# u and v rows of a mixture of experts side by side: one 8 KB gather per choice for three of four token tiles

## The chip, the cores and the metric

One core of a Trainium2 chip. The time is device microseconds of one execution, median over runs: 4290.01 us (4275.37, 4290.01, 4290.02).

## The reference

Two transformer blocks on 512 tokens of width 1024; the second ends with a layer of single experts (PEER), which is all that the change touches. For a tile of 128 tokens:

```
q = t @ wq                          # per head, two halves of 128
v1,i1 = top_k(q1 @ k1.T, 16); v2,i2 = top_k(q2 @ k2.T, 16)
score, ci = top_k(v1[:,None]+v2[None,:], 16)       # of 256 sums
expert = i1[ci // 16] * 128 + i2[ci % 16]          # one of 16384
w = softmax(score) * gelu(u_tab[expert] . t)       # u_tab: 16384 x 1024
y = sum over 8 heads x 16 choices of w * v_tab[expert]
```

So each token has 128 choices, and each choice reads one row of 1024 f32 (4 KB) of u and one of v. After it come a scaled residual and a layer norm.

## The kernel before

It is one program per engine, with the order written out by hand and semaphores between engines. Each stage names its steps (`pe.V.at("dot", n)` is "VectorE has finished step dot n of stage peer"). The 512 tokens are four tiles; tile 0 is prepared (attention output, merge, norm, query product, selection) while the last attention runs, tiles 1 to 3 together behind it.

`FETCH` (L2502) is the order of all 1024 row gathers, and also the order of work: `("pu", i, j)` is u row of choice j of tile i, `("pv", i, j)` its v row. Tile 0's first 64 u rows go alone, then one v row comes per four u rows, and from u row 128 on five v rows per four u rows, until the v rows have caught up. So tile 1's u rows run beside tile 0's v rows, and v rows trail u rows by up to 112.

A gather (L2752, on POOL's queue) brings one row per partition, 128 rows of 4 KB, 512 KB, into one of `PLACES`: 7 places for the first 144 gathers, then 19 (12 more in the panels of the weight w_pq+, free once the query product of tiles 1 to 3 is done). It waits until the last row of that place is used: a u row by its dot, a v row by its matmuls.

`in_order` (L2670) is run by every engine with its own parts: at each row r it first issues the gathers whose places come free by r (on POOL), waiting with `advance` while the selection of their head isn't `ready`, then does the row's own work, then `advance(r)`: 2 steps of the selection for r < 128, later 2 and 1 in turn, and from r >= 30 on every third turn one step of the rest of the tail for tiles 1 to 3 (`others`).

- VectorE, u row (L2782): one multiply and sum of the row with the token tile (the dot). After 16 of them five small instructions make the gelu's polynomial, and ScalarE's sigmoid stands between them (L2715, L2792).
- ScalarE, v row (L2721): a diagonal 128x128 of the weights w, in one of 4 buffers.
- TensorE, v row (L2705): diagonal times row, two halves of 512 columns, summed in PSUM; the profile shows four matmuls of 128x512 f32 per v row.
- Selection on VectorE (L2609 to L2664): some 27.5 steps per head, among them L2611 (needs ScalarE's copy of the scores, L2586) and the softmax (needs L2592). The query product of tiles 1 to 3 is L258, 16 groups of 16 matmuls.
- At each tile's last v row (L2802) VectorE makes the residual and the norm.

Of the kernel before, what the change touches and what calls it, by code (L numbers as in the profile page):

```python
# [8 lines left out]
U32 = mybir.dt.uint32  # L9
# [90 lines left out]
def build(nc, d, out):  # L100
    ctx = ExitStack()
    with ctx:
# [2398 lines left out]
        BL = 16  # L2501
        FETCH = []  # L2502
        done_v = 0
        for n_ in range(1, 513):
            FETCH.append(("pu", (n_ - 1) // 128, (n_ - 1) % 128))
            goal = 0 if n_ < 64 else (n_ - 64) // 4 if n_ < 128 else 16 + (n_ - 128) * 5 // 4 if n_ < 512 else 512
            while done_v < goal:
                FETCH.append(("pv", done_v // 128, done_v % 128))
                done_v += 1
        ROWS = len(FETCH)  # L2510
        PLACES = [piece(o_cs + 1024), piece(o_ka + 1024), piece(o_ka + 2048), piece(o_cs), MIXf[:, 0:1024], piece(o_ht + 1024), piece(o_ka)]
        FEW = len(PLACES)
        PLACES += [panel("w_pq+", c)[:, 1024 * j:1024 * j + 1024] for c in (1, 2, 3) for j in range(4)]
        MANY = len(PLACES)
        FROM = 144
        SPOT = [n % FEW if n < FROM else (n - FROM) % MANY for n in range(ROWS)]
        NTH, PREV, uses, user_row = [], [], [0] * MANY, [-1] * MANY
        for n_ in range(ROWS):
            uses[SPOT[n_]] += 1
            NTH.append(uses[SPOT[n_]])  # L2520
            PREV.append(user_row[SPOT[n_]])
            user_row[SPOT[n_]] = n_
        NUMBER = {f: n for n, f in enumerate(FETCH)}
        s_row_in = [sem(f"s_in{j}") for j in range(MANY)]

        def fetched(f):
            return s_row_in[SPOT[NUMBER[f]]], 16 * NTH[NUMBER[f]]

        def row(f):
            return PLACES[SPOT[NUMBER[f]]]  # L2530

# [6 lines left out]
        EXU = [piece(o_end + 128 * j, 128).bitcast(U32) for j in range(4)]  # L2538
        DOT = [piece(o_end + 512 + 128 * j, 128) for j in range(2)]
# [69 lines left out]
        def select_vector(v, asked, ready):  # L2609
# [12 lines left out]
            for i in range(4):  # L2622
                for h in range(8):
# [11 lines left out]
                    pe.V.own(v).tensor_copy(I1F, I1).then_inc(*pe.V.step())  # L2635
# [4 lines left out]
                    for half in (0, 1):  # L2640
# [3 lines left out]
                        else:  # L2644
# [10 lines left out]
                                                     op1=ALU.add).then_inc(*pe.V.step("sel", i, h))  # L2655
                    yield
# [13 lines left out]
        def in_order(e, part, select, gather=lambda n: None):  # L2670
# [12 lines left out]
            for r in range(ROWS):  # L2683
                while n < ROWS and PREV[n] < r:
                    tab, i, j = FETCH[n]
                    while tab == "pu" and (i, j // 16) not in ready:
                        advance(r)
                    gather(n)
                    n += 1
                yield FETCH[r]  # L2690
                advance(r)
# [35 lines left out]
        YY, XHR = MIXf[:, 1024:2048], MIXf[:, 2048:3072]  # L2727
        s_late, s_xhr = sem("s_late"), sem("s_xhr")

        def rows_gpsimd(g):  # L2730
            def gather(n):
                tab, i, j = FETCH[n]
                if PREV[n] >= 0:
                    tab0, i0, j0 = FETCH[PREV[n]]
# [4 lines left out]
                elif SPOT[n] in (1, 2):  # L2739
                    g.wait_ge(*tl.V.at("rows"))  # L2740
                elif SPOT[n] == 3:
                    g.wait_ge(*tl.V.at("bias"))
                elif SPOT[n] == 4:
                    g.wait_ge(*tl.P.at("mx", 0, 1))
                elif SPOT[n] == 5:
                    g.wait_ge(*tl.P.at("o", 0, 1, 0))
                elif SPOT[n] == 6:
                    g.wait_ge(s_xh[0], 16)
                elif SPOT[n] >= FEW:
                    g.wait_ge(*tl.P.at("q", 1, 4 * (1 + (SPOT[n] - FEW) // 4) + 3))  # L2750
                g.wait_ge(*pe.V.at("sel", i, j // 16))
                g.indirect_dma_start(PLACES[SPOT[n]], None, d[tab], bass.IndirectOffsetOnAxis(ap=EXU[i][:, j:j + 1], axis=0)  # L2752
                                     ).then_inc(s_row_in[SPOT[n]], 16)
# [3 lines left out]
            for f in in_order(g, tail_gpsimd, select, gather):  # L2757
                if f == ("pv", 0, 24):
# [320 lines left out]
```

## Time and profile before

| | |
|---|---|
| median of 3 runs | 4290.01 us |
| profiled execution: span from first to last instruction | 4287.8 us |
| TensorE busy | 3534.2 us (82%) |
| VectorE busy | 2141.1 us (50%) |
| POOL busy | 1437.5 us (34%) |
| gathers: 512 u rows, 512 v rows | mean 1070 and 1100 ns on POOL |
| dots (L2782) | 512, mean 1221 ns |
| matmuls of v rows (L2705) | 2048, 1029.6 us |

The page gives no other time for the profiled execution than its span. Shares are means over stages with different limits; the slices and the tables by stage show which engine is full where.

### The profile page before, as it was taken

How to read it: one execution, taken by the hardware profiler on the slowest of the kernel's cores; microseconds unless marked ns; L12 is line 12 of the kernel's file. 1: busy time of each engine (PE TensorE's matmuls, PEld its weight loads, DVE VectorE, ACT ScalarE, POOL GpSimd, SP SyncE). 2: the span in 40 equal slices, each digit the busy share in tenths (PEclk: the TensorE clock that was granted, in tenths of full speed). 3: DMA queues.
4: the chain of work that ended last, by engine and by line, in shares of the span. 5: the costliest groups of instructions: out<-in, count | busy, mean ns of one | idle time of the engine just before them, and what ended most of it. 6: DMA issues, size and time to landing. Idle time of an engine off the chain costs nothing.

```text
span 4287.8 us, 33127 instructions
## 1 busy us (share of the span) xinstructions
PE 3534.2 (82%) x10814; PEld 1820.1 (42%) x10814; DVE 2141.1 (50%) x4648; ACT 910.5 (21%) x1890; POOL 1437.5 (34%) x1337
## 2 busy tenths in 40 slices
PE   8377999999997999979999875678777777777776
PEld 4244544444453564456544563234333333333232
DVE  0557234421013567746344458764678776334432
ACT  1234411000032225622110322111122212111111
POOL 0214400000000006400000023354777776777774
PEclk9668999999999989979899987889898898988998
DMA  3010111333211113201212456675998999999996
GB/s 153 8 50 1 57 62 69 157 149 129 95 59 54 59 54 106 81 35 62 101 39 98 154 188 224 236 281 200 375 350 324 353 369 334 366 371 363 369 360 244
DMA packets 171912, 765.15 MB, mean 178 GB/s; under 512 B 19256, under 2 KB 19256, under 8 KB 160224
## 3 DMA queue, kind: packets, MB, share of 16 engines
q0 software_dynamic: 157904, 580.06, 36.8%
q1 hardware_dynamic: 13824, 182.97, 11.4%
q8 instruction: 88, 1.44, 0.1%
q14 instruction: 80, 0.66, 0.0%
q10 hardware_dynamic: 16, 0.02, 0.0%
HBM read 744.08 MB, written 18.89 MB: 178 GB/s over the span
## 4 chain that ended last, share of the span: by engine, by line
PE 50%; DVE 18%; issue 10%; POOL 5%; DMA 3%; ACT 3%; another core or an unknown queue 2%; POOLq 0%; DVEq 0%; ACTq 0%
PE ps L252 14%; PE ps L258 11%; DVE arena L2782 7%; PE ps L1416 6%; PE ps L1346 5%; POOL arena L2752 4%; PE ps L2705 4%; PE ps L1722 2%; PE ps L220 2%; DMA arena<-in_pu,arena 1%; DMA arena<-in_pv,arena 1%; PE ps L1709 1%; DVE arena L2613 1%; DVE arena L2619 1%
## 5 line engine op out<-in xcount | busy, mean ns | idle before, releaser
L2705 PE MATMUL ps<-arena 128*128 128x512 f32 x2048 | 1029.6, 658 | 395.5 <-issue 195.0
L2705 PEld LDWEIGHTS ps<-arena 128*128 128x128 f32 x2048 | 411.3, 208 | 991.1 <-issue 881.0
L2782 DVE CUSTOM_DVE_ANT_0 arena<-arena 128x1024 f32<-128x1024 f32 x512 | 622.6, 1221 | 367.3 <-DMA arena<-in_pu,arena 337.6
L252 PE MATMUL ps<-arena 128*128 128x512 f32 (+1 forms) x1768 | 755.9, 588 | 32.0 <-ACT arena L2271 24.4
L2752 POOL DMA_INDIRECT arena<-in_pu,arena x512 | 547.7, 1070 | 422.7 <-issue 98.1
L2752 POOL DMA_INDIRECT arena<-in_pv,arena x512 | 563.1, 1100 | 204.3 <-issue 127.1
L258 PE MATMUL ps<-arena 128*128 128x512 f32 (+2 forms) x1408 | 529.5, 537 | 3.1 <-DVE arena L1263 0.9
L252 PEld LDWEIGHTS ps<-arena 128*128 128x128 f32 x1768 | 337.9, 192 | 435.7 <-issue 430.6
L258 PEld LDWEIGHTS ps<-arena 128*128 128x128 f32 x1408 | 267.6, 191 | 262.0 <-issue 216.8
L220 PE MATMUL ps<-arena 128*128 128x128 f32 x1046 | 194.5, 321 | 206.0 <-ACT arena L812 49.8
L2721 ACT ACTIVATE arena<-arena 128x128 f32<-128x128 f32 x512 | 192.8, 397 | 751.1 <-PE ps L2705 360.6
L1416 PE MATMUL ps<-arena 128*128 128x512 f32 x640 | 293.6, 606 | 20.1 <-ACT arena L1802 12.8
L263 POOL TENSOR_TENSOR arena<-arena 128x1 f32<-128x1 f32 (+7 forms) x38 | 61.3, 1615 | 722.7 <-DVE arena L630 311.0
L220 PEld LDWEIGHTS ps<-arena 128*128 128x128 f32 x1046 | 141.1, 163 | 288.8 <-issue 146.7
L1440 POOL DMA_DIRECT2D aside<-arena x20 | 10.7, 534 | 661.5 <-ACT arena L1430 661.5
L1346 PE MATMUL ps<-arena 128*128 128x512 f32 x512 | 221.5, 593 | 1.4 <-DVE arena L1380 1.4
L1416 PEld LDWEIGHTS ps<-arena 128*128 128x128 f32 x640 | 118.6, 194 | 147.7 <-issue 129.4
L1072 POOL TENSOR_SCALAR arena<-arena 128x128 f32<-128x128 f32 (+3 forms) x96 | 111.3, 1170 | 157.6 <-DVE arena L1103 89.0
L1246 POOL DMA_DIRECT2D x_spill<-arena x1 | 0.6, 573 | 463.8 <-DVE arena L1377 463.8
L1346 PEld LDWEIGHTS ps<-arena 128*128 128x128 f32 x512 | 96.7, 190 | 125.7 <-issue 123.4
L1722 PEld LDWEIGHTS ps<-arena 128*128 128x128 f32 x896 | 119.0, 209 | 30.6 <-issue 17.2
L1722 PE MATMUL ps<-arena 128*128 128x64 f32 x896 | 118.1, 289 | 5.9 <-DVE arena L1918 5.8
(342 smaller groups left out, 3399.5 us busy)
## 6 DMA issues: line engine op xcount, KB each, us to landing
arena<-in_w_in SPq DMA_DIRECT2D x27, 2048.0 KB, 8.9
arena<-in_w_ada SPq DMA_DIRECT2D x12, 2048.0 KB, 8.0
arena<-in_w_ff_in SPq DMA_DIRECT2D x8, 2048.0 KB, 12.5
arena<-in_w_ff_out SPq DMA_DIRECT2D x8, 2048.0 KB, 12.5
arena<-in_w_pq SPq DMA_DIRECT2D x8, 2048.0 KB, 8.5
aside<-arena POOLq DMA_DIRECT2D x20, 512.0 KB, 4.5
arena<-in_w_at SPq DMA_DIRECT2D x4, 2048.0 KB, 8.9
arena<-in_w_o SPq DMA_DIRECT2D x4, 2048.0 KB, 8.7
```

The costliest lines, as they stand in the source:

```text
L220: return t.transpose(ps, src, ID[0:src.shape[0], 0:src.shape[0]])
L252: x = t.matmul(PS[:, b, 0:n], hT[:, k, i * 128:(i + 1) * 128], w[:, k, :], start=k == 0, stop=k == nk - 1)
L258: x = t.matmul(PS[:, b, 0:n], w[:, k, f * 128:(f + 1) * 128], hT[:, k, 0:n], start=k == 0, stop=k == nk - 1)
L263: return g.tensor_tensor(o, o, MH[0:o.shape[0], 0:o.shape[-1]], ALU.pow)
L1072: g.tensor_scalar(probs(i, h), probs(i, h), r[:, 6 + h:7 + h], None, ALU.mult).then_inc(*at1.G.step("scaled", i, h))
L1346: x = t.matmul(PS[:, 4 * c + i, :], AT[:, 8 * kk + k, 128 * i:128 * i + 128], w[:, k, :], start=kk == 0 and k == 0, stop=kk == 3 and k == 7)
L1416: x = t.matmul(PS[:, b, :], l, r, start=k == 0, stop=k == 7)
L1722: x = t.matmul(PS[:, b, 64 * c:64 * c + 64].rearrange("p (n t) -> p n t", t=w), WL[lv % 4][:, o:o + 128], sides(WL[lv % 4][:, o:o + 128], ...
L2705: x = t.matmul(PS[:, b + c, :], DG[n % 4], row(f)[:, 512 * c:512 * c + 512], start=j == 0, stop=j == 127)
L2721: a.activation(DG[n % 4], ID, ACT.Copy, scale=GS[i][:, j:j + 1]).then_inc(*pe.A.step("dg", n))
L2752: g.indirect_dma_start(PLACES[SPOT[n]], None, d[tab], bass.IndirectOffsetOnAxis(ap=EXU[i][:, j:j + 1], axis=0)).then_inc(s_row_in[SPOT[n]] ...
L2782: v.tensor_tensor_reduce(row(f), row(f), TT[i], 1.0, 0.0, ALU.mult, ALU.add, DOT[i % 2][:, j:j + 1]).then_inc(*pe.V.step("dot", 128 * i + j))
```

## The change

- The tables are laid side by side (`uv`, 16384 rows of 2048 f32). For tiles 1 to 3 one gather per choice brings the 8 KB row into one of 14 places of 8 KB (`PAIRS`): u in the first half, v in the second. For tile 0 the same table is seen as 32768 rows of 4 KB (`HALVES`), u at index 2e, v at 2e + 1 (`EXV`), in 7 places (`CELLS`).
- The order is now a list of work (`WORK`), apart from the list of gathers: tile 0's u rows with v rows as before up to u row 127, then its remaining 112 v rows alone, then for tiles 1 to 3 u row n and v row n - 10 (`LAG`) in turn. There are 256 + 384 = 640 gathers. A place of 8 KB is freed by the v row's matmuls. Eight of the 14 places lie on regions that tile 0's places or other buffers use, with waits for their last users.
- The gelu blocks are 8 choices for tiles 1 to 3 (16 for tile 0), with one small instruction fewer.
- Some waits and loads beside it move to other rows (late rows at v row 80 and 112 of tile 0, residual at 116 instead of 100), and two buffers move.

```diff
-        BL = 16
-        FETCH = []
...
-            goal = 0 if n_ < 64 else (n_ - 64) // 4 if n_ < 128 else 16 + (n_ - 128) * 5 // 4 if n_ < 512 else 512
...
-        FROM = 144
-        SPOT = [n % FEW if n < FROM else (n - FROM) % MANY for n in range(ROWS)]
...
+        BLOCK = (16, 8, 8, 8)
+        LAG = 10
+        UV = d["uv"]
+        HALVES = UV.rearrange("e (s n) -> (e s) n", s=2)
+        WORK = []
+        done_v = 0
+        for n_ in range(1, 129):
+            WORK.append(("pu", 0, n_ - 1))
+            while done_v < (n_ - 64) // 4:
+                WORK.append(("pv", 0, done_v))
+                done_v += 1
+        WORK += [("pv", 0, j_) for j_ in range(done_v, 128)]
+        for n_ in range(384 + LAG):
+            if n_ < 384:
+                WORK.append(("pu", 1 + n_ // 128, n_ % 128))
+            if n_ >= LAG:
+                WORK.append(("pv", 1 + (n_ - LAG) // 128, (n_ - LAG) % 128))
...
+        PAIRS = [panel("w_pq+", c)[:, 2048 * j:2048 * j + 2048] for c in (1, 2, 3) for j in range(2)]
+        PAIRS += [piece(o, 2048) for o in (o_va + 1024, o_ka + 2048, o_qa + 2048, o_ka, o_cs, W0, o_t + 2048, o_ht)]
+        MANY = len(PAIRS)
+        SHARED = {7: (2,), 9: (6, 1), 10: (3, 0), 11: (4,), 13: (5,)}
+        FETCH = [f for f in WORK if f[1] == 0]
+        SPOT = [n % FEW for n in range(256)]
+        FETCH += [("uv",) + f[1:] for f in WORK if f[1] and f[0] == "pu"]
+        SPOT += [FEW + n % MANY for n in range(384)]
...
@@ selection, vector @@
+                    if i == 0:
+                        pe.V.own(v).tensor_scalar(EXV[:, hs], EXU[0][:, hs], 1, None, ALU.add).then_inc(*pe.V.step("selv", h))
@@ in_order @@
-                while n < ROWS and PREV[n] < r:
+                while n < FETCHES and FREED[n] < r:
...
-                    while tab == "pu" and (i, j // 16) not in ready:
+                    while tab != "pv" and (i, j // 16) not in ready:
@@ gather @@
+                if i == 0:
+                    g.wait_ge(*(pe.V.at("sel", 0, j // 16) if tab == "pu" else pe.V.at("selv", j // 16)))
+                    x = (EXU[0] if tab == "pu" else EXV)[:, j:j + 1]
+                    g.indirect_dma_start(CELLS[k], None, HALVES, bass.IndirectOffsetOnAxis(ap=x, axis=0)).then_inc(s_row_in[k], 16)
+                else:
+                    g.wait_ge(*pe.V.at("sel", i, j // 16))
+                    g.indirect_dma_start(PAIRS[k - FEW], None, UV, bass.IndirectOffsetOnAxis(ap=EXU[i][:, j:j + 1], axis=0)
+                                         ).then_inc(s_row_in[k], 16)
@@ rows_vector @@
+                        pe.V.own(v).scalar_tensor_tensor(out=y, in0=x, scalar=0.044715, in1=x, op0=ALU.mult, op1=ALU.mult
+                                                         ).then_inc(*pe.V.step())
+                        pe.V.own(v).scalar_tensor_tensor(out=y, in0=y, scalar=1.0, in1=x, op0=ALU.add, op1=ALU.mult
+                                                         ).then_inc(*pe.V.step("poly", i, j // bl))
@@ layout @@
-    a["pu"] = i["peer_u_2"][0]
-    a["pv"] = i["peer_v_2"][0]
+    a["uv"] = np.concatenate([i["peer_u_2"][0], i["peer_v_2"][0]], 1)
```

## Rows read from the trace of the kernel before

**Rows 1.** The page: DMA's busy tenths in 40 slices of 107.2 us.

```profile
DMA  3010111333211113201212456675998999999996
```

**Rows 2.** Window, us, busy us (x) of PE PEld DVE ACT POOL, clock, DMA share, GB/s.

```profile
2519.00:2891.00 372.00, 231.06 (x744) 129.22 (x745) 287.67 (x709) 65.29 (x133) 164.21 (x155) 0.81 0.72 244
2891.00:2964.00 73.00, 67.24 (x194) 36.01 (x193) 22.53 (x66) 12.19 (x27) 16.66 (x17) 1.00 0.32 108
...
3300.00:3600.00 300.00, 230.54 (x507) 99.16 (x506) 226.08 (x651) 61.29 (x157) 226.07 (x203) 0.89 0.95 353
3600.00:3900.00 300.00, 229.78 (x464) 92.24 (x462) 126.30 (x220) 47.50 (x126) 221.23 (x208) 0.88 0.97 363
3900.00:4245.00 345.00, 254.80 (x517) 100.87 (x516) 137.50 (x245) 51.16 (x137) 252.27 (x241) 0.91 0.97 364
```

**Rows 3.** The same windows for the gathers alone (L2752): POOL busy (count).

```profile
2519.00:2891.00 372.00, 157.55 (x144) 0.81 0.72 244
...
3600.00:3900.00 300.00, 220.04 (x206) 0.88 0.97 363
3900.00:4245.00 345.00, 251.10 (x239) 0.91 0.97 364
```

**Rows 4.** Timeline of POOL, unheld: start us, us, what [idle before <-releaser].

```profile
3532.43 0.94 POOL L2752 DMA_INDIRECT arena<-in_pu,arena  x1 [0.30 <-issue]
```

**Rows 5.** As rows 2: 16 KB rows (5:25), then 4 KB rows; the weight loads.

```profile
5.00:25.00 20.00, 10.44 (x44) 7.63 (x45) 5.92 (x9) 6.73 (x12) 1.02 (x1) 1.00 1.02 428
3000.00:3050.00 50.00, 34.81 (x69) 14.75 (x70) 29.24 (x84) 7.26 (x18) 35.07 (x34) 0.80 1.01 394
4100.00:4200.00 100.00, 71.82 (x148) 27.16 (x146) 41.31 (x75) 12.88 (x36) 73.96 (x72) 0.94 1.00 380
...
arena<-in_w_in SPq DMA_DIRECT2D x27, 2048.0 KB, 8.9
```

**Rows 6.** Timelines of POOL and of PE around the 144th gather.

```profile
2891.61 0.95 POOL L2752 DMA_INDIRECT arena<-in_pu,arena  x1 [7.96 <-DVE arena L2658]
...
2962.55 0.95 POOL L2752 DMA_INDIRECT arena<-in_pu,arena  x1 [25.94 <-PE ps L258]
...
2890.64 26.03 PE L258 MATMUL ps<-arena 128*128 128x384 f32 x80
```

**Rows 7.** DVE by line, 3300 to 3600 us; first and last of six dots.

```profile
L2782 DVE CUSTOM_DVE_ANT_0 arena<-arena 128x1024 f32<-128x1024 f32 x94 | 114.1, 1216 | 3.2 <-DMA arena<-in_pu,arena 2.3 <-issue 0.9
L2611 DVE MAX8 arena<-arena 128x8 f32<-128x128 f32 (+1 forms) x32 | 11.0, 342 | 44.0 <-ACT arena L2586 25.8 <-issue 14.6 <-remote 1.9
...
3427.97 1.21 DVE L2782 CUSTOM_DVE_ANT_0 arena<-arena 128x1024 f32<-128x1024 f32 x1
...
3440.99 1.22 DVE L2782 CUSTOM_DVE_ANT_0 arena<-arena 128x1024 f32<-128x1024 f32 x1
```

**Rows 8.** v rows on PE: L2705's matmuls to 2880 us; timelines at 2889, 3780.

```profile
2519.00:2880.00 361.00, 42.06 (x56) 13.50 (x56) 0.81 0.73 246
...
2888.85 1.95 PE L2705 MATMUL ps<-arena 128*128 128x512 f32 x4 [0.96 <-ACT arena L2721]
...
3779.95 3.75 PE L2705 MATMUL ps<-arena 128*128 128x512 f32 x4 [6.10 <-issue]
3784.21 25.04 PE L2705 MATMUL ps<-arena 128*128 128x512 f32 x56 [0.51 <-issue]
```

**Rows 9.** Timeline of the end: last gather, v rows, last DVE step.

```profile
4244.17 0.95 POOL L2752 DMA_INDIRECT arena<-in_pv,arena  x1 [0.30 <-issue]
...
4248.70 25.98 PE L2705 MATMUL ps<-arena 128*128 128x512 f32 x56 [1.98 <-ACT arena L2721]
...
4282.90 1.23 DVE L2815 TENSOR_TENSOR arena<-arena 128x1024 f32<-128x1024 f32 x1
```

**Rows 10.** A wait, 3300 to 3600 us (total, times, longest); the queues' instruction packets.

```profile
ACT arena L2586 <- remote: 37.2, 3, 21.1
...
q8 instruction: 88, 1.44, 0.1%
```

More of the change, by code:

```diff
@@ new lines, in build, with number, emptied @@
+        for n_ in range(FETCHES):
+            k_ = SPOT[n_]
+            PREV.append([held_by[k_]] if uses[k_] else [held_by[c] for c in SHARED.get(k_ - FEW, ())])
+            uses[k_] += 1
+            NTH.append(uses[k_])
+            held_by[k_] = FETCH[n_]
+        NUMBER = {f: n for n, f in enumerate(FETCH)}
+        s_row_in = [sem(f"s_in{j}") for j in range(FEW + MANY)]
+        def number(f):
+            return NUMBER[f if f[1] == 0 else ("uv",) + f[1:]]
+        def emptied(f):
+            return ("pu" if f[0] == "pu" else "pv",) + f[1:]
@@ L2526, in fetched @@
+        FREED = [max((WHEN[emptied(f)] for f in before), default=-1) for before in PREV]
         def fetched(f):
-            return s_row_in[SPOT[NUMBER[f]]], 16 * NTH[NUMBER[f]]
+            return s_row_in[SPOT[number(f)]], 16 * NTH[number(f)]
         def row(f):
-            return PLACES[SPOT[NUMBER[f]]]
+            n = number(f)
+            if f[1] == 0:
+                return CELLS[SPOT[n]]
+            o = 1024 * (f[0] == "pv")
+            return PAIRS[SPOT[n] - FEW][:, o:o + 1024]
@@ L2634, in select_vector @@
                     pe.V.named["used", i, h] = pe.V.n
-                    pe.V.own(v).tensor_copy(I1F, I1).then_inc(*pe.V.step())
+                    if i:
+                        pe.V.own(v).tensor_copy(I1F, I1).then_inc(*pe.V.step())
+                    else:
+                        pe.V.own(v).tensor_scalar(I1F, I1, 2.0, None, ALU.mult).then_inc(*pe.V.step())
                     v.tensor_tensor(CD.rearrange("p (a b) -> p a b", a=16), bc(V1[:, 0, :], 16), rep(V1[:, 1, :], 16), ALU.add
@@ L2732, in gather @@
                 tab, i, j = FETCH[n]
-                if PREV[n] >= 0:
-                    tab0, i0, j0 = FETCH[PREV[n]]
+                k = SPOT[n]
+                for tab0, i0, j0 in PREV[n]:
                     if tab0 == "pu":
@@ L2738, in gather @@
                         g.wait_ge(*pe.P.at("add", 128 * i0 + j0))
[L2739 to L2750, printed above, removed]
@@ L2751, in gather @@
-                g.wait_ge(*pe.V.at("sel", i, j // 16))
-                g.indirect_dma_start(PLACES[SPOT[n]], None, d[tab], bass.IndirectOffsetOnAxis(ap=EXU[i][:, j:j + 1], axis=0)
-                                     ).then_inc(s_row_in[SPOT[n]], 16)
+                if NTH[n] == 1:
+                    if k in (1, 2):
+                        g.wait_ge(*tl.V.at("rows"))
+                    elif k == 3:
+                        g.wait_ge(*tl.V.at("bias"))
+                    elif k == 4:
+                        g.wait_ge(*tl.P.at("mx", 0, 1))
+                    elif k == 5:
+                        g.wait_ge(*tl.P.at("o", 0, 1, 0))
+                    elif k == 6:
+                        g.wait_ge(s_xh[0], 16)
+                    elif k >= FEW:
+                        g.wait_ge(*tl.P.at("q", 1, (7, 7, 11, 11)[k - FEW] if k < FEW + 4 else 15))
+                    if k == FEW + 8:
+                        g.wait_ge(s_xh[1], 16)
+                        g.wait_ge(s_xh[2], 32)
+                    elif k == FEW + 12:
+                        g.wait_ge(*tl.V.at("tt", 3))
+                        g.wait_ge(*pe.V.at("dot", 127))
+                    elif k == FEW + 13:
+                        g.wait_ge(*pe.P.at("sc", 0, 3))
@@ L2797, in rows_vector @@
                     v.tensor_scalar(LATE[3], LATE[3], ALPHA, None, ALU.mult).then_inc(*pe.V.step())
-                if f and tab == "pv" and j == 100:
+                if f and tab == "pv" and j == 116:
                     v.wait_ge(s_xhr, 16 * (i + 1))
```

56 lines of the change are left out of this document (24 added, 32 removed).

## The prediction

> **What bounds the kernel now.** I read the page's slices first [rows 1]: DMA's tenths go from 5 to 7 up to 9 for the last 12 slices, from about 3000 us. So the last 1.3 ms are bound near DMA, and only the gathers that fill them are touched by the change. The table by stage [rows 2] gives the four stages: to 2891 us tile 0's u rows (DMA share 0.72); 2891 to 2964 with DMA at 0.32; then both tiles' rows with the selection beside them, DMA 0.95 and the vector engine (DVE) 0.75 busy; from 3600 DMA 0.97 and DVE only 0.40 to 0.42. The gathers by stage [rows 3]: 144 before 2891 us, then 880 until the last at 4244 us [rows 9], 1.54 us each with the hole at the start, and 1.45 us each after 3600 (445 in 645 us), that is 2.90 us for the two rows of a choice.
>
> Why not faster? Two things are close together. POOL needs 1.25 us per gather (0.94 and 0.30 between) when nothing holds it [rows 4], and 512 KB at the highest rate that gathers reach over 50 us (394 GB/s, a few plain loads among them) is 1.33 us [rows 5]. A POOL that is held for a few us can therefore never catch up. The hole at 2891: the gather after the 144th wants tile 1's first choices, which the order puts before tile 0's remaining v rows, and POOL waits for the selection (7.96 us) and for TensorE's query product (25.94 us) [rows 6]. In the third stage DVE, which works through choices in a fixed order, is the pace: 94 dots in 300 us, 3.19 us each, with almost no wait for DMA (3.2 us) but 44.0 us at L2611 for the score copy [rows 7].
>
> **The change part by part.** Up to the 144th gather nothing moves except 8 small DVE instructions (the v indices) and one fewer per block, about 0.2 us each: 2891 us stays.
>
> *A, tile 0's v rows by themselves.* 112 v rows now stand in a row with no dot beside them, and TensorE is what is busy. Before 2890.6 us it had done 15 v rows (56 matmuls up to 2880, 4 more at 2889, four a row) [rows 8]; to v row 120, whose place lets the first 8 KB gather start, 106 remain. A row costs 1.78 us back to back (56 matmuls in 25.04), 1.96 alone [rows 8]: 106 x 1.78 = 189. The query product of tiles 1 to 3 still has 10 groups of 16 matmuls (five take 26.03, 5.2 each) [rows 6], 52 us, a gap of 1 us at each (0.96 in [rows 8]), and I allow 4 us for score matmuls: 255 us, so v row 120 is done at 3146. DMA (106 x 1.33 = 141 us) and POOL hide beneath. The hole at 2891 goes, since no choice of tile 1 is asked for in this stretch; by the turn counts, 1.5 selection steps a row make 6 of tile 1's 8 heads ready by then. With 1.95 a row it is 3164, the upper end; the lower is 3141.
>
> *B, choices while DVE still selects.* DVE must first finish tile 0's end (12 us of v rows left, then its chain, 4274.7 to 4284.1 in the last tile [rows 9]): 3168. The selection of tiles 1 to 3 has 24 heads x 27.5 = 660 steps. Tile 1's first query product is asked for about row 135, and 1.5 steps in each of the 120 rows from there do 180. The other 480 come at 1.5 a turn: one turn in each of the first 10 choices, two in the others, so 155 more choices carry three steps each. In the packed stretch six dots start 2.60 us apart, with 3.4 steps each [rows 7]: the dot with its read-out 1.26, so a step 0.40. A choice is then 1.26 + 3 x 0.40 = 2.46, and a block of 8 adds 4 small instructions and the wait for the sigmoid, 1.7 us, 0.21 a choice: 2.67. Ten light choices at 1.9 and 155 at 2.67 end at 3168 + 19 + 414 = 3601. This is above DMA's pace (below), so DVE is the bound there. Lower end 2.5 (no waits); upper 3.19, as now, if the waits at L2611 stay.
>
> *C, the rest.* Fourteen places less the ten choices between a dot and its v row leave three or four 1 MB transfers in flight. DMA is then about 2 choices ahead of DVE: 217 remain. No row shows an indirect row of 8 KB. From one side: TensorE's weights come in rows of 16 KB (2048 KB over 128 partitions) at 428 GB/s [rows 5], 2.45 us for 1 MB. From the other: the rate of 4 KB rows with the chip's queues full, 394 and 380 GB/s [rows 5], 2.66 and 2.76; the average now is 2.90 [rows 3]. A price per row and one per byte fitted to 394 and 428 (256 rows a MB in 2.66 us, 64 in 2.45, so 128 in 2.52) say 2.52; I take 2.55. POOL has 1.25 us of work in that time and stops being a partner in the bound. Places: after block b's last dot its v rows start some 4 us later and take 8 x 1.98 us (229.78 us for 464 matmuls, four a row [rows 2]); the gather for the first freed place must be out within 6 x 2.55 = 15 us and is out after 8 or 9, the last within 33 and out after 22. So depth is enough at this clock. 217 x 2.55 = 553: last row lands at 4154; the tiles' residual loads, output stores and two tile ends add 8 (six transfers of 512 KB at 1.3 us): 4162.
>
> *The end.* Now the last gather goes out at 4244.2, but TensorE is 15 v rows behind and ends at 4274.7 [rows 9], and 13.1 us follow. Then: dot 1.3, small work 2, 8 v rows (first at half clock, 3.75, the rest 1.78) 16.2, and 13.1: 33 us. 4162 + 33 = 4195.
>
> *Waits for nothing in the program.* ACT stood 21.1 us at L2586 for a release that the profile can't name, with DVE behind it [rows 7, 10]; a small queue of instruction packets runs beside the gathers (88 packets) [rows 10]. Such waits were inside the 3.19, not in my 2.67: I add 20 us, between none and 40. The Trainium skill (Runtime: NRT & Kernel Launch, Instruction fetch mechanics) says the refill of instructions in 16 KiB blocks is mostly hidden; by that the 20 would be 0. The 21.1 us wait speaks against it, though no row proves that a refill is its cause.
>
> **Sum: span 4215**, against 4287.8: 73 us less (-1.7%). The median of the runs is 4290.0, 2.2 above the profiled span; 4217 in that measure.
>
> The Trainium skill (DMA: Bandwidth & Descriptors, Where 436 GB/s comes from) puts the limit from HBM to one core at about 358 GB/s; by that 1 MB takes 2.93 us and the change loses, an end near 4336 (3150 + 384 x 2.93 + 61, an estimate from that page). The rows exceed it already (394 and 428 [rows 5]); rival 4 is the same as a mechanism of this kernel, from rows.
>
> **Rivals.**
> 1. *An 8 KB row costs two 4 KB rows* (it travels as two packets, or HBM rather than a fixed price per row is the limit): 2.76 us a choice throughout. 3150 + 384 x 2.76 = 4210, with the same 8 + 33 + 20 = 61 behind it 4271, 4273 measured: hardly any gain, since stage A has given away 95 us of DMA time. For it: 380 and 394 leave little under 428, and waits included the two are near. Against: 16 KB rows at 428. 0.16.
> 2. *DVE's pace stays 3.19 with its waits.* 155 x 0.52 = 81 us more, less the 20 already added: 4276, 4278 measured. For it: L2611's 44.0 us [rows 7]. Against: TensorE has one v row per choice and not 1.25, so the score matmul should be there when DVE comes. 0.11.
> 3. *Slower: TensorE falls to its lower clock in the gaps between blocks.* After a gap of 6.10 us a v row took 3.75 us, the 1.2 GHz level, not 1.78 [rows 8]. With blocks of 8 the wait for the block's weights comes twice as often. Places are released at the v row's pace, so TensorE is the bound once more than 0.4 of the v rows run at the lower level (8 x (1.78 + 0.4 x 1.97) = 20.5 us, DMA's time for 8). At 0.6 a choice takes 2.96 us: 3150 + 384 x 2.96 + 61 = 4348. Against: the granted clock now is 0.88 to 0.91 at the same load [rows 2]. 0.06.
> 4. *Slower: memory gives no more than the mean rate of now*, 353 to 364 GB/s [rows 2, 3], 2.90 us a choice, whatever the row's length: 3150 + 384 x 2.90 + 61 = 4325. It decides from 2.76 us a choice on, where the gain of stage C has gone. Against: 428 and 394 in [rows 5]. 0.03.
>
> **How the numbers follow.** My forecast has 0.64. Its own spread: stage A 3141 to 3164, DVE at 2.5 to 2.9, DMA at 2.45 to 2.66 after it, unnamed waits 0 to 40, together 4148 to 4260. The range of 8 in 10 reaches up to rivals 1 and 2: 4158 to 4292. A measurement of this kernel tells 0.5% (21 us) from nothing: faster is below 4268.5, same up to 4311.5. Faster: 0.62 of the forecast's 0.64, half of rival 1 and a fifth of rival 2, 0.72. Slower: rivals 3 and 4 and a little of 2, 0.11. Same 0.17.
>
> **What would show it.** In the profile after: first 8 KB gather near 3150 us and TensorE over 0.9 busy from 2891 to it (A); dots 2.6 to 2.8 us apart, DVE over 0.9 busy, until about 3600 (B); then DMA share 1.0 at 400 GB/s or more and dots 2.55 apart (C); last gather at 4150 to 4175. Wrong if the rate in C stays at 380 or less (rival 1), if L2611's idle stays above 8 us per head pair (2), if the granted clock drops under 0.8 (3), or if v row 120 ends after 3180.

## The result, and the profile after

The changed kernel takes 4352.97 us (median of four runs) against 4290.02 for the kernel before (4275.37 to 4294.05): a ratio of 1.0151 with a 95% interval of [1.0121, 1.018]. One run of this kernel (5068.87 us) and one of e2 below (8322.63 us) were slow for a reason that no trace shows; they count in the medians, but not in the ratios or the ranges given (here 4348.22 to 4357.32, with a median of 4348.61). The kernel is slower by 1.5% where 4217 and a gain of 1.7% were predicted; the time lies outside the range of 4158 to 4292. The profiled span is 4346.8 us against the 4215 of the sum.

The page after, its slices of DMA (answers to [rows 1]) and the costliest groups that belong to the change:

```profile
DMA  3010112333211122201213368675898888998996
GB/s 152 8 49 1 59 58 91 132 155 135 94 42 53 67 72 89 98 30 59 97 39 142 128 199 276 216 246 189 307 359 339 361 333 344 361 362 328 369 361 241
...
L2832 DVE CUSTOM_DVE_ANT_0 arena<-arena 128x1024 f32<-128x1024 f32 x512 | 624.6, 1221 | 403.7 <-DMA arena<-in_uv,arena 403.1
...
L2802 POOL DMA_INDIRECT arena<-in_uv,arena x384 | 429.0, 1117 | 698.7 <-PE ps L2739 351.5
...
L2799 POOL DMA_INDIRECT arena<-in_uv,arena x256 | 264.7, 1034 | 387.7 <-PE ps L2739 146.3
...
L2750 ACT ACTIVATE arena<-arena 128x8 f32<-128x8 f32 (+1 forms) x56 | 11.8, 211 | 613.0 <-DVE arena L2840 613.0
```

The last 12 slices, nearly all 9 before, are mostly 8, at 328 to 369 GB/s but for the last one. The dots (L2832) wait 403 us for rows. POOL, which issues the 8 KB rows (L2802), waits most for v rows of TensorE (L2739, 351.5 of 698.7 us), that is for places. So the engine before the DMA and the engine behind it both wait, and the DMA is still not full: a loop is held somewhere. The last row is a clue: ScalarE stands 613 us at one line, the sigmoid of a block (L2750), waiting for that block's last dot.

The windows after (as [rows 2]):

```profile
2891.00:3150.00 259.00, 241.59 (x607) 113.11 (x606) 67.29 (x246) 48.49 (x135) 107.78 (x116) 0.99 0.68 231
3150.00:3300.00 150.00, 92.95 (x191) 40.06 (x190) 112.21 (x308) 30.25 (x70) 58.29 (x52) 0.78 0.88 348
3300.00:3600.00 300.00, 203.13 (x433) 87.61 (x431) 241.25 (x679) 66.31 (x155) 115.92 (x101) 0.86 0.89 349
3750.00:3900.00 150.00, 105.46 (x210) 44.62 (x209) 65.25 (x124) 18.57 (x56) 57.00 (x54) 0.83 0.91 358
3900.00:4050.00 150.00, 104.22 (x193) 43.38 (x192) 71.99 (x130) 18.82 (x56) 51.26 (x50) 0.78 0.88 339
```

In the first window TensorE is busy 241.59 of 259 us. From 3150 us DMA, TensorE and DVE are all below full. In 3750 to 3900 the DMA share is 0.91 at 358 GB/s, less than with 4 KB rows (0.97, 363 [rows 2]). The timeline of the first 8 KB rows on POOL and of the end (answers to [rows 6] and [rows 9]):

```profile
3153.01 0.95 POOL L2799 DMA_INDIRECT arena<-in_uv,arena  x1 [0.77 <-PE ps L2739]
3154.26 0.95 POOL L2802 DMA_INDIRECT arena<-in_uv,arena  x1 [0.30 <-issue]
...
4299.77 0.94 POOL L2802 DMA_INDIRECT arena<-in_uv,arena  x1 [0.77 <-PE ps L2739]
...
4310.78 1.22 DVE L2832 CUSTOM_DVE_ANT_0 arena<-arena 128x1024 f32<-128x1024 f32 x1
...
4313.10 20.87 PE L2739 MATMUL ps<-arena 128*128 128x512 f32 x44 [8.45 <-ACT arena L2757]
```

The 384 gathers of 8 KB take 4299.8 - 3154.3 = 1145.5 us, 2.98 us each; two 4 KB gathers took 2.90 in the last stage before.

**The loop, read from one block.** The timeline of the kernel after around the end of a block of 8 choices (start, duration, engine and line, idle before and what ended it):

```profile
3782.39 1.86 POOL L2802 DMA_INDIRECT arena<-in_uv,arena  x1 [0.78 <-PE ps L2739]
...
3788.45 1.23 DVE L2832 CUSTOM_DVE_ANT_0 arena<-arena 128x1024 f32<-128x1024 f32 x1 [1.26 <-DMA arena<-in_uv,arena]
...
3790.12 0.21 ACT L2750 ACTIVATE arena<-arena 128x8 f32<-128x8 f32 x1 [14.37 <-DVE arena L2840]
3790.24 1.26 ACT L2757 ACTIVATE arena<-arena 128x128 f32<-128x128 f32 x4
...
3790.76 15.77 PE L2739 MATMUL ps<-arena 128*128 128x512 f32 x32 [8.64 <-ACT arena L2757]
3790.95 1.23 DVE L2832 CUSTOM_DVE_ANT_0 arena<-arena 128x1024 f32<-128x1024 f32 x1 [0.42 <-DMA arena<-in_uv,arena]
...
3793.43 1.23 DVE L2832 CUSTOM_DVE_ANT_0 arena<-arena 128x1024 f32<-128x1024 f32 x1 [1.25 <-DMA arena<-in_uv,arena]
...
3794.78 0.94 POOL L2802 DMA_INDIRECT arena<-in_uv,arena  x1 [10.53 <-DVE arena L2832]
...
3795.89 1.23 DVE L2832 CUSTOM_DVE_ANT_0 arena<-arena 128x1024 f32<-128x1024 f32 x1 [1.23 <-DMA arena<-in_uv,arena]
...
3800.32 1.23 DVE L2832 CUSTOM_DVE_ANT_0 arena<-arena 128x1024 f32<-128x1024 f32 x1 [3.19 <-DMA arena<-in_uv,arena]
```

The dot at 3788.45 is the last of its block. ScalarE has waited 14.37 us for it; it makes the sigmoid and at once four diagonals (L2757), TensorE starts after 8.64 us of idle, its v rows free places, and POOL issues at 3794.78 after 10.53 us. (The profile puts that wait down to a dot, L2832; the gather's code waits for the v row's matmuls alone, and the first four of these ended at 3794.51.) In between exactly three more rows arrive (dots at 3790.95, 3793.43, 3795.89, 2.5 us apart), and the fourth only 4.43 us later.

The first v row behind the pause takes 3.75 us (3790.76 to 3794.51), since TensorE runs at its lower clock then; back to back at the higher one it takes 1.8 [rows 8]. The windows show it (columns as in [rows 2]):

```profile
3792.00:3794.50 2.50, 2.50 (x4) 0.94 (x4) 1.25 (x3) 0.00 (x0) 0.00 (x0) 0.53 0.91 380
3794.50:3797.00 2.50, 2.50 (x8) 1.06 (x7) 1.27 (x3) 0.80 (x2) 1.44 (x2) 1.00 0.33 59
```

Over the 20 whole blocks between 3620 and 4120 us the eight distances between dots, from one block's last dot on, are on average 2.55, 2.45, 3.18, 4.36, 2.94, 3.07, 2.73 and 2.55: 23.8 us a block, where eight at 2.48 would take 19.8. DMA around the block shown, in 40 slices of 0.35 us:

```profile
DMA  9999999999999999973100009169999998999999
GB/s 468 398 398 445 421 445 398 421 445 421 398 445 398 445 421 421 375 304 140 47 23 0 0 0 281 47 211 351 398 398 421 445 398 351 421 398 421 445 445 421
```

This is the window 3788 to 3802: full at some 420 GB/s, empty around 3795 to 3797, full again.

Why four diagonals at once? ScalarE makes its instructions in one list. With ten choices between a dot and its v row, that list has, ahead of the last choice of block b, the v rows up to 8b-4. The sigmoid of block b comes next, and then the v rows 8b-3, 8b-2, 8b-1, which belong to the block before and whose weights had long been there. They stand behind a wait that they don't need. Their places come free only after the block's last dot, so of 14 places only 14 - 8 - 3 = 3 can carry rows beyond it. The trace bears it out: in all 20 blocks exactly three gathers have been issued beyond the row of the block's last dot when that dot starts. Of the four diagonals, three are these. This is **theory 1**. The rivals: **theory 2**, an 8 KB row is no faster than two 4 KB rows; **theory 3**, TensorE at its lower clock behind the pause between the blocks.

### The profile page after: what moved, and what is told of

The parts are those of the page before. It is cut to its first block, busy times and chain, and to the rows that moved or that the text cites. A ratio compares the mean times of both kernels' runs of the same rounds, so it can differ in the third digit from the quotient of the medians.

```text
span 4346.8 us, 32494 instructions
## 1 busy us (share of the span) xinstructions
PE 3543.2 (82%) x10814; PEld 1840.9 (42%) x10814; DVE 2157.1 (50%) x4720; ACT 915.8 (21%) x1924; POOL 1019.3 (23%) x953
## 3 DMA queue, kind: packets, MB, share of 16 engines
q1 hardware_dynamic: 13824, 182.97, 11.3%
## 4 chain that ended last, share of the span: by engine, by line
PE 52%; DVE 14%; DMA 11%; issue 7%; POOL 4%; ACT 3%; POOLq 0%; DVEq 0%; ACTq 0%
PE ps L252 13%; PE ps L258 12%; DMA arena<-in_uv,arena 11%; DVE arena L2832 6%; PE ps L1416 6%; PE ps L2739 5%; PE ps L1346 5%; POOL arena L2802 3%; PE ps L1722 2%; PE ps L220 2%; PE ps L1709 1%; PE ps L786 1%; PE ps L1031 1%; PE ps L2330 1%; PE ps L768 1%
## 5 line engine op out<-in xcount | busy, mean ns | idle before, releaser
L2739 PE MATMUL ps<-arena 128*128 128x512 f32 x2048 | 1033.2, 665 | 451.0 <-ACT arena L2757 427.6
L2739 PEld LDWEIGHTS ps<-arena 128*128 128x128 f32 x2048 | 428.7, 214 | 1034.1 <-issue 972.0
L2832 DVE CUSTOM_DVE_ANT_0 arena<-arena 128x1024 f32<-128x1024 f32 x512 | 624.6, 1221 | 403.7 <-DMA arena<-in_uv,arena 403.1
L2802 POOL DMA_INDIRECT arena<-in_uv,arena x384 | 429.0, 1117 | 698.7 <-PE ps L2739 351.5
L252 PEld LDWEIGHTS ps<-arena 128*128 128x128 f32 x1768 | 338.2, 193 | 436.0 <-issue 431.0
L258 PEld LDWEIGHTS ps<-arena 128*128 128x128 f32 x1408 | 267.7, 191 | 262.9 <-issue 218.7
L2799 POOL DMA_INDIRECT arena<-in_uv,arena x256 | 264.7, 1034 | 387.7 <-PE ps L2739 146.3
L2757 ACT ACTIVATE arena<-arena 128x128 f32<-128x128 f32 x512 | 183.7, 393 | 377.3 <-PE ps L2739 345.4
L220 PEld LDWEIGHTS ps<-arena 128*128 128x128 f32 x1046 | 142.3, 164 | 283.6 <-issue 162.5
L1416 PEld LDWEIGHTS ps<-arena 128*128 128x128 f32 x640 | 118.6, 194 | 147.7 <-issue 129.5
L1346 PEld LDWEIGHTS ps<-arena 128*128 128x128 f32 x512 | 96.7, 190 | 125.7 <-issue 123.4
L2750 ACT ACTIVATE arena<-arena 128x8 f32<-128x8 f32 (+1 forms) x56 | 11.8, 211 | 613.0 <-DVE arena L2840 613.0
L1722 PEld LDWEIGHTS ps<-arena 128*128 128x128 f32 x896 | 119.0, 209 | 30.6 <-issue 17.7
## 6 DMA issues: line engine op xcount, KB each, us to landing
arena<-in_w_ff_in SPq DMA_DIRECT2D x8, 2048.0 KB, 12.4
```

Of the source, the lines that this page charges most:

```text
L220: return t.transpose(ps, src, ID[0:src.shape[0], 0:src.shape[0]])
L252: x = t.matmul(PS[:, b, 0:n], hT[:, k, i * 128:(i + 1) * 128], w[:, k, :], start=k == 0, stop=k == nk - 1)
L258: x = t.matmul(PS[:, b, 0:n], w[:, k, f * 128:(f + 1) * 128], hT[:, k, 0:n], start=k == 0, stop=k == nk - 1)
L1346: x = t.matmul(PS[:, 4 * c + i, :], AT[:, 8 * kk + k, 128 * i:128 * i + 128], w[:, k, :], start=kk == 0 and k == 0, stop=kk == 3 and k == 7)
L1416: x = t.matmul(PS[:, b, :], l, r, start=k == 0, stop=k == 7)
L1722: x = t.matmul(PS[:, b, 64 * c:64 * c + 64].rearrange("p (n t) -> p n t", t=w), WL[lv % 4][:, o:o + 128], sides(WL[lv % 4][:, o:o + 128], ...
```

## The experiments

All ratios are to the kernel before, on the same chip. That kernel's median was 4292.58 us beside e1 to e4, 4291.86 beside e5 to e7, and 4277.96 beside e8 and e9, so times across these groups are compared by their ratios. For each kernel one window is shown, 3750 to 4050 us, and the dots in it. The kernel after:

```profile
3750.00:4050.00 300.00, 209.68 (x402) 87.99 (x401) 137.23 (x254) 37.39 (x112) 108.26 (x103) 0.81 0.90 349
```

Its group by line, in the same stretch:

```profile
L2832 DVE CUSTOM_DVE_ANT_0 arena<-arena 128x1024 f32<-128x1024 f32 x98 | 120.0, 1227 | 152.3 <-DMA arena<-in_uv,arena 152.3
```

**e1_diagonals_first**: the three diagonals ahead of the sigmoid, all else as in the kernel after (`diagonal(n)` is the old code for one v row, which also notes n in `made`; the old place skips what is made).

```diff
+                    if tab == "pu" and i and j % bl == bl - 1:
+                        for n in range(max(128, 128 * i + j - LAG), 128 * i + j - bl + 1):
+                            diagonal(n)
                     if tab == "pu" and j % bl == bl - 1:
                         a.wait_ge(*pe.V.at("poly", i, j // bl))
...
```

> The changed kernel with one thing moved on ScalarE: at a block's end it makes the diagonals of the last v rows of the block before (3 of them at a lag of 10) before the block's sigmoid, not behind it. Theory 1 (the sigmoid, which waits for the block's last dot, holds back three v rows whose weights are long ready, so their places come free late and only 3 transfers are in flight past the last dot; DMA runs dry once per block of 8): DMA share 0.97 or more in 3750 to 4150, dots there 2.5 to 2.6 us apart and not 2.99, time about 4220 (4200 to 4260). Theory 2 (8 KB rows from memory are no faster than the 360 GB/s that the profile shows): no change, 4340 to 4365. Theory 3 (TensorE's half clock after each gap sets the pace): v rows still come in bursts, so under 20 us less, 4330 to 4353.

Measured 4222.78 us (4221.14 to 4225.06), ratio 0.9838 [0.9822, 0.9854].

```profile
3750.00:4050.00 300.00, 233.97 (x466) 98.68 (x465) 162.43 (x304) 46.16 (x134) 134.47 (x120) 0.85 1.00 413
```

Its group by line, in the same stretch:

```profile
L2842 DVE CUSTOM_DVE_ANT_0 arena<-arena 128x1024 f32<-128x1024 f32 x117 | 143.3, 1226 | 131.3 <-DMA arena<-in_uv,arena 131.3
```

Three instructions of ScalarE change their order in each block, nothing else, and 130 us go: DMA is full, 413 GB/s, and 117 dots stand where 98 stood. This confirms theory 1: at a block's last dot six gathers are out beyond it in 19 of 23 blocks.

**e2_lag7**: seven choices between dot and v row, so that no v row of the block before is left behind the sigmoid.

```diff
-        LAG = 10
+        LAG = 7
```

> The changed kernel with LAG 7 in place of 10: no v row of the block before then stands behind the sigmoid of a block of 8. Theory 1: the same gain as with the diagonals first, about 4220 (4200 to 4260), dots 2.5 to 2.6 us apart after 3700. Theory 2: 4340 to 4365. Theory 3: bursts of 8 v rows behind each block remain, 4330 to 4353.

Measured 4215.6 us (4212.7 to 4216.35), ratio 0.9815 [0.9796, 0.9835], span 4214.5.

```profile
3750.00:4050.00 300.00, 234.65 (x471) 98.89 (x470) 163.47 (x306) 46.85 (x135) 136.53 (x120) 0.87 1.00 414
...
3900.00:4050.00 150.00, 120.31 (x241) 50.57 (x240) 77.89 (x152) 23.55 (x69) 68.28 (x62) 0.87 1.01 421
```

Its timeline:

```profile
3799.21 0.21 ACT L2750 ACTIVATE arena<-arena 128x8 f32<-128x8 f32 x1 [9.88 <-DVE arena L2840]
...
3804.12 0.94 POOL L2802 DMA_INDIRECT arena<-in_uv,arena  x1 [7.04 <-PE ps L2739]
```

The same result by another way. The timeline rows teach a limit of such a reading: ScalarE still waits 9.88 us and POOL 7.04, but with six rows in flight beyond the block these waits cost nothing. 421 GB/s refutes theory 2 as to the row's rate. Theory 3 falls too as what sets the pace by itself: TensorE still pauses once a block, its first v row behind the pause still takes 3.5 us on average, and a choice takes 2.5 us.

**e3_lag12**: the same line with 12, which puts five v rows behind the sigmoid and leaves one in flight.

> LAG 12: five v rows of the block before stand behind the sigmoid and only one transfer is in flight past the block's last dot. Theory 1: the first released choice lands 11.9 us after the last dot's row as now, then 6 more at 2.48 us, 26.8 us per block instead of 21.8, and with the 2 us that the mean of now lies above that 3.6 us a choice: 384 x 0.6 = 230 us more, about 4580 (4500 to 4620). Theory 2: no change, 4340 to 4365. Theory 3: the same bursts with longer gaps, a few tens of us more, 4370 to 4420.

Measured 4662.88 us (4654.2 to 4677.5), ratio 1.0855 [1.0836, 1.0873].

```profile
3750.00:4050.00 300.00, 167.44 (x326) 70.57 (x324) 119.37 (x274) 35.87 (x99) 81.40 (x81) 0.78 0.71 270
```

The direction is theory 1's; the loss is larger, by 83 us, than it expected, and the time lies outside its range (4500 to 4620). The pace after the first 165 choices is 3.60 us a choice, as foreseen (3.6), but while DVE still selects it is 4.1 (673.2 us for 165). That the waits for rows and the steps of the selection, which follow the rows' order, add up there is likely, but no run shows it.

**e4_lag7_two_gathers**: as e2, but each choice is fetched by two gathers of 4 KB into the halves of the same place.

```diff
-                    g.indirect_dma_start(PAIRS[k - FEW], None, UV, bass.IndirectOffsetOnAxis(ap=EXU[i][:, j:j + 1], axis=0)
-                                         ).then_inc(s_row_in[k], 16)
+                    for o, x in ((0, EXU[i]), (1024, EXV[i])):
+                        g.indirect_dma_start(PAIRS[k - FEW][:, o:o + 1024], None, HALVES, bass.IndirectOffsetOnAxis(ap=x[:, j:j + 1], axis=0)
+                                             ).then_inc(s_row_in[k], 16)
...
```

> LAG 7, and the 8 KB of a choice of tiles 1 to 3 come as two gathers of 4 KB rows into the same place (the indices 2e and 2e + 1, 8 more small DVE instructions per tile). It tells what the 8 KB row gives by itself. If the row's length matters as the packets of the trace suggest (POOL 2 x 1.25 us, 4 KB rows at 394 GB/s at best): 2.7 to 2.9 us a choice where the 8 KB row has 2.5, so 40 to 80 us more than with LAG 7 and one gather, 4260 to 4300. If bytes alone count: within 15 us of LAG 7 with one gather.

Measured 4339.45 us (4335.13 to 4346.6), ratio 1.0105 [1.0088, 1.0121].

```profile
3750.00:4050.00 300.00, 210.23 (x408) 87.49 (x409) 141.91 (x265) 41.58 (x119) 211.70 (x204) 0.83 0.94 357
```

Its group by line, in the same stretch:

```profile
L2799 POOL DMA_INDIRECT arena<-in_uv,arena x202 | 210.8, 1044 | 88.6 <-issue 54.4 <-PE ps L2735 14.8 <-remote 12.3
```

So the 8 KB row by itself is worth 4339.45 - 4215.6 = 124 us, 2.9%, more than the 40 to 80 expected. POOL issues 202 gathers in 300 us, 1.49 us each, with 54.4 us of its idle ended by nothing but its own issuing; DMA is at 0.94. The new order of the work (at seven choices) with 4 KB rows is 1% slower than the kernel before. How much of it is POOL's and how much the DMA's own rate for 4 KB rows, this run does not separate.

**e5_lag9**: the same line with 9, two v rows behind the sigmoid, four in flight.

> LAG 9, between 7 (4216) and 10 (4353): two v rows stand behind the sigmoid, four transfers in flight past the last dot. By the same sum as before (first released choice lands 11.9 us after the last dot's row, then 3 more at 2.48: 19.3 us, under the 19.8 us that 8 choices take on DMA) the hole is just closed: 4225 to 4250. If instead what counts is that any v row stands behind the sigmoid, and each costs alike (137 us for three), it is near 4307.

Measured 4269.91 us (4262.19 to 4280.99, 10 runs), ratio 0.9958 [0.994, 0.9975].

```profile
3750.00:4050.00 300.00, 223.78 (x436) 94.32 (x437) 152.43 (x286) 42.80 (x128) 124.62 (x108) 0.85 0.97 386
```

A miss by 20 us: four in flight (the trace has exactly four in all 22 blocks) don't close the hole (386 GB/s).

**e9_lag7_12_places**: seven choices (`LAG = 7`, as in e2), but 12 places: no v row behind the sigmoid, and 12 - 8 = 4 in flight, as in e5.

```diff
+        PAIRS = PAIRS[:12]
```

> LAG 7 with 12 places of 8 KB in place of 14. If the number of transfers in flight past a block's last dot is what sets the pace (places - 8 with nothing held back: 4, the same number as LAG 9 with 14 places: 13 - 9), the time is that of LAG 9: 4270 (4250 to 4290). If only what stands behind the sigmoid counts: 4216, as with 14 places.

Measured 4277.52 us (4267.47 to 4282.08, 10 runs), ratio 0.9993 [0.9979, 1.0006].

```profile
3750.00:4050.00 300.00, 211.24 (x424) 89.10 (x422) 149.41 (x281) 42.07 (x122) 120.23 (x108) 0.86 0.96 377
```

Two ways to four in flight give 377 and 386 GB/s: the number of rows that can travel past the block's last dot goes far to set the pace, whatever takes the others. The two are near each other, not equal: their ratios, 0.9993 and 0.9958, lie apart by more than their intervals, and what makes the last 0.35% is not shown.

**e6_lag7_selection_spread**: e2, and from tile 1's first choice on (row 256 of `WORK`, behind the 128 u and 128 v rows of tile 0) one selection step a turn instead of three in two turns, so that what is left of the selection spreads into the stretch that DMA bounds.

```diff
-                drain(chosen, 2 if r < 128 or turns[0] % 2 else 1)
+                drain(chosen, 2 if r < 128 or (r < 256 and turns[0] % 2) else 1)
```

> LAG 7, and from row 256 on the selection advances one step per turn and not 2 and 1 in turn: two steps a choice, so that it lasts some 240 choices and not 155. If VectorE's work is the bound while it selects (my stage B: dot 1.26, steps 0.40 each): a choice takes 1.26 + 0.8 + 0.2 = 2.3 us on VectorE, below DMA's 2.5, so DMA is the bound all through: some 35 us less than LAG 7 alone, 4180 (4165 to 4195). If the slower dots of that stretch (2.75 us) come from something else, such as the waits for an unnamed release: 4205 to 4220.

Measured 4172.91 us (4168.18 to 4176.14), ratio 0.9733 [0.9711, 0.9756]. Two groups of DVE in 3300 to 3600 us in e2:

```profile
L2832 DVE CUSTOM_DVE_ANT_0 arena<-arena 128x1024 f32<-128x1024 f32 x105 | 127.4, 1213 | 0.0
...
L2640 DVE MAX8 arena<-arena 128x8 f32<-128x128 f32 (+1 forms) x33 | 11.2, 341 | 22.2 <-ACT arena L2615 20.9
```

The same window in e6:

```profile
3300.00:3600.00 300.00, 231.15 (x498) 99.12 (x497) 246.51 (x646) 70.89 (x171) 138.57 (x120) 0.89 0.99 409
```

Its group by line, in the same stretch:

```profile
L2832 DVE CUSTOM_DVE_ANT_0 arena<-arena 128x1024 f32<-128x1024 f32 x117 | 142.9, 1222 | 25.7 <-DMA arena<-in_uv,arena 25.5 <-issue 0.2
```

In e2 no dot waits for a row (0.0): DVE was the bound while it selected. In e6 the dots wait 25.5 us for DMA, which is at 0.99 and 409 GB/s, and the first 165 choices take 413.6 us where e2 took 451.2. This version beats both kernels, by 2.7% and by about 4%.

**e7_spread_early_rows**: e6, and the first seven rows of tile 1 are fetched after 212 of tile 0's 256 gathers, and their dots put between tile 0's last v rows, one per four, where DMA has room (0.68 in the first window after).

> As the run before, and the first 7 rows of tile 1 are fetched in the stretch of tile 0's v rows, where DMA is idle a third of the time (their places are free by then), with their dots one per 4 v rows from v row 100 on. DMA has 7 x 2.5 us less to do after that stretch: 17 us less than the run before, 4163 (4150 to 4180). If TensorE's stretch grows by as much, or the tile's end hides it: no change.

Measured 4177.53 us (4176.22 to 4178.51), ratio 0.9747 [0.9726, 0.9767]: inside its range, but no gain over e6, which is the second reading of the expectation. POOL's first and last early gather and the next gather for tile 0, then PE, in the stretch that TensorE bounds:

```profile
3065.09 0.95 POOL L2806 DMA_INDIRECT arena<-in_uv,arena  x1 [0.30 <-issue]
...
3072.61 0.94 POOL L2806 DMA_INDIRECT arena<-in_uv,arena  x1 [0.30 <-issue]
3073.86 0.95 POOL L2803 DMA_INDIRECT arena<-in_uv,arena  x1 [0.30 <-issue]
...
3089.18 7.25 PE L2743 MATMUL ps<-arena 128*128 128x512 f32 x12 [11.33 <-DMA arena<-in_uv,arena]
3100.70 9.60 PE L2743 MATMUL ps<-arena 128*128 128x512 f32 x15 [4.26 <-DMA arena<-in_uv,arena]
```

The seven early rows stand in the DMA queue ahead of tile 0's v rows, and TensorE waits 15.6 us for these, where e6 waits 4.0 us for DMA in this stretch: what was won later is paid here.

**e8_lag12_diagonals_first**: e3's 12 choices with e1's order (five diagonals ahead of the sigmoid).

> LAG 12, with the five diagonals of the block before made ahead of the sigmoid. It parts the two readings of the lag: if a long lag costs because ScalarE's sigmoid stands before diagonals (theory 1), order alone gives back all of the 447 us that LAG 12 costs against LAG 7: 4215 to 4245. If it costs because places are held from a dot to its v row for more choices (places less lag): near 4600, as with LAG 12 alone.

Measured 4272.57 us (4266.54 to 4277.81, 10 runs), ratio 0.9985 [0.9972, 0.9998]. The two windows:

```profile
3750.00:4050.00 300.00, 229.34 (x462) 96.69 (x461) 159.79 (x296) 45.65 (x131) 131.79 (x117) 0.86 0.98 407
...
3300.00:3600.00 300.00, 184.92 (x405) 81.28 (x404) 228.40 (x648) 66.07 (x150) 103.79 (x94) 0.80 0.82 327
```

The order alone gives back 390 of the 447 us between e2 and e3 (4662.88 - 4272.57; by the ratios, 0.087 of 0.104), and after the selection it is about as fast as e2 (407 GB/s). It misses its range by 28 us, and that is in the stretch of the selection (327 GB/s, e2 373): the first 165 choices take 502.9 us, in e2 451.2. ScalarE's waits in that stretch begin with this row (total, times, longest; in e2 it has 68.2, 10, 11.3):

```profile
ACT arena L2621 <- DVE arena L2692: 94.1, 9, 15.8
```

L2621 is a step of the selection; it can stand ahead of diagonals as the sigmoid did. That was not tried and stays open.

Window 3750 to 4050 of all, by the number of rows that can be in flight past a block's last dot (places less the block's 8 less those held):

| kernel | in flight | dots | us a dot | GB/s | time, us |
|---|---|---|---|---|---|
| e3, 12 choices | 1 | 76 | 3.95 | 270 | 4662.9 |
| after, 10 choices | 3 | 98 | 3.06 | 349 | 4353.0 |
| e9, 12 places | 4 | 108 | 2.78 | 377 | 4277.5 |
| e5, 9 choices | 4 | 110 | 2.73 | 386 | 4269.9 |
| e8, 12 choices, order | 6 | 115 | 2.61 | 407 | 4272.6 |
| e1, order | 6 | 117 | 2.56 | 413 | 4222.8 |
| e2, 7 choices | 6 | 118 | 2.54 | 414 | 4215.6 |

(Us a dot is 300 us over the dots; e3 still selects in this window, which makes its figure larger than its pace of 3.60 afterwards. In the traces the count at a block's last dot is 3 in all 20 blocks of the kernel after and 4 in all 22 of e5 and of e9; it is 1 in 14 of 15 blocks of e3, and 6 in 21 of 23 of e2, 19 of 23 of e1 and 18 of 23 of e8. Five in flight was not tried.)

## Why the prediction was wrong

The step that failed is **Places, in C**: "after block b's last dot its v rows start some 4 us later and take 8 x 1.98 us [...]; the gather for the first freed place must be out within 6 x 2.55 = 15 us". It goes wrong twice.

The 6 is wrong. It takes all 14 places with only the block's 8 held, but the order of ScalarE's list holds three more v rows behind the sigmoid, and 3 are in flight. The prediction itself gives "three or four 1 MB transfers in flight" at the start of C and didn't put the two numbers side by side. And the test asks when the gather must be out, not when its row must be there: the way from issue to dot beyond the transfer, 5.5 - 2.5 = 3 us, is put at nothing. With 3 in place of 6 the test asks for 7.4 us, which the prediction's own "8 or 9" miss, but which the measured 6.3 still pass.

What the runs show in its place: three rows last 3 x 2.48 = 7.4 us beyond the last dot, and a fourth would be due at 9.9. The first new row needs 3794.78 - 3788.45 = 6.3 us to be issued and 5.5 more to its dot at 3800.32, 11.9 us in all. That is the 2 us too many at the fourth distance; the other 2 us of a block lie at its neighbours (3.18, 2.94, 3.07 above), where the queue is likely short before and after. Of the 6.3 us, 2 are the lower clock of the first v row (3.75 us and not 1.8), so that clock is a part of the way; whether three in flight would do without it was not tried.

By this sum alone four in flight (12.4 us) would do, and e5 shows that they don't (21.8 us a block over 22 blocks): its fifth row's dot starts 13.7 us after the last dot on average, and why is open. With six (17.4 us to the seventh) the margin is enough: e2's blocks take 20.4 us. The 3.4 us of difference over C's 27 blocks are 92 us, and C took 644.9 - 554.9 = 90 us less.

Term by term (start times of dots and gathers in the traces, us):

| term | predicted | after | e2 |
|---|---|---|---|
| A: first 8 KB gather | 3150 | 3154.3 | 3157.1 |
| first dot of tile 1 | 3168 | 3174.6 | 3177.4 |
| B: 165 choices beside the selection | 433 | 491.3 | 451.2 |
| C: the rest, to the last dot | 553 + 8 | 644.9 | 554.9 |
| the end | 33 | 36.0 | 31.1 |
| unnamed waits | 20 | none of DVE | none of DVE |
| span | 4215 | 4346.8 | 4214.5 |

- **A was right.** TensorE was the bound (241.59 of 259 us at a clock of 0.99), and the first 8 KB gather came 4 us after the forecast. That this stage gives away time of the DMA was right too, and e7 shows that it isn't easily had back.
- **B: the bound was right, with the hole on top.** DVE is the bound once the order is mended: 451.2 us in e2, 2.73 a choice. That this is so near to 433 and the 20 of unnamed waits is in part luck: no wait of DVE in that stretch is unnamed, and DVE stands 24.3 us at L2640 for ScalarE's copy of the scores, which the 2.67 a choice left out. In the kernel after the hole costs 40 us more, and its dots wait 47.3 us for rows. Waits in B (total, times, longest), the first of the kernel after, the others of e2:

```profile
DVE arena L2832 <- DMA arena<-in_uv,arena: 47.3, 48, 3.2
...
DVE arena L2640 <- ACT arena L2615: 24.3, 7, 4.8
...
DVE arena L2832 <- DMA arena<-in_uv,arena: 0.5, 1, 0.5
```

- **Rival 2** (3.19) did not come: L2640's idle is 22.2 us in 3300 to 3600 us of e2, half of the 44.0 of L2611 before [rows 7].
- **C: the row's price was right, the supply was not.** 2.48 us between dots when DMA is full, against 2.55 taken and 2.66 to 2.76 of rival 1. The loss of 84 us is the hole.
- **The end was right** to 3 us. Of **unnamed waits** there is no sign in C (e2's 554.9 against 561 without them).
- **Rival 3** names the measured time best (4348), and its sign, a granted clock under 0.8, stands in two windows above (0.78). As a cause by itself it is refuted by e1 and e2: a pause per block is still there, the clock is 0.85 to 0.87, and DMA is full. The rival also makes TensorE the bound, and it was busy 105.46 of 150 us. In the kernel after the 32 matmuls behind a pause of 8.64 us take 15.77 us, in e2 15.40 behind 3.10 us. What it has right is the slow first v row, which e1 and e2 have as well (3.6 and 3.5 us on average), and which costs nothing with six in flight.
- **Rival 1**'s sign, a rate in C of 380 or less, was met too (349 GB/s), and e2's 421 GB/s refutes the rival: neither sign could tell its rival from a held loop.
- **Rival 4** gave nearly the measured time (4325 against a span of 4346.8) for the wrong reason: its rate, 2.90 us a choice, is what a held loop happened to give, and e2 shows memory at 421 GB/s. The limit of 358 GB/s from HBM to one core (the Trainium skill, DMA: Bandwidth & Descriptors, Where 436 GB/s comes from) would have given 4336 as an estimate, close as well; by the 421 of e2 this kernel is not held by it. A time that fits is not a cause shown.

Where the 1.5% comes from, in factors: the order of the work without 8 KB rows 1.0105 (e4); the 8 KB row 0.9815 / 1.0105 = 0.971; three v rows behind the sigmoid 1.0151 / 0.9815 = 1.034. The change's idea was worth its 1.8%, and one list on one engine took it and more.

## What to carry to other kernels

When buffers circulate (gather, dot, weights, v row, free), count the transfers that can be in flight at the worst moment, not on average: places, less the block, less every step that is ready but stands in its engine's list behind a wait for something later; multiply by the time of one transfer and compare with the way from the last dot to the next arrival. Leave a margin: here four fell short although the sum allowed them, and six were enough. An engine that works in order and waits once a block for the newest data is the place to look; move what is ready ahead of that wait, or choose the distance so that nothing ready is left behind. And an engine idle for 7 us a block proves nothing: e2 has such waits with a full DMA, and only the DMA's share tells the difference.

## What the hardware showed that was not expected

- Indirect gathers of 8 KB rows (128 a transfer) run at 421 GB/s with the DMA share at 1.01 over 150 us, near the 428 of plain 16 KB rows [rows 5]; gathers of 4 KB reached 380 to 394 there (with a few plain loads among them at 394).
- An indirect gather costs POOL the same for 4 and 8 KB rows: 0.95 us and 0.30 to the next. The rows at 3153 and 3154 us above and [rows 4] show it for 4 KB, e7's seven early gathers of 8 KB, 1.25 us apart (3065.09 to 3072.61), for 8 KB. With the queues full some take longer (0.94 to 1.95 us; mean 1117 ns for 8 KB against 1034 for 4 KB on the page).
- When the DMA has run dry or nearly, 5.5 us pass from the issue of a 1 MB gather to the start of its dot (3794.78 to 3800.32), of which 2.5 are the transfer at full rate. It came back in each block: the median is 5.7 us over the 20 blocks of the kernel after and 5.6 over 15 of e3.
- TensorE's first v row behind a pause took 3.75 us at a granted clock of 0.5, the lower level of 1.2 GHz, in most blocks of the kernel after (pause 6.8 us on average) and in half of e2's (4.5 us). Back to back at the higher level it takes 1.8 [rows 8].
